# Order of the fillers at the opening of a gather-bound kernel, half of a top-64 moved among the first dots, and one unit's query products eight picks later

## The reference, cut to what matters

```
q = (h @ w_query)                          # 8 heads x 2 halves x 128
s1, s2 = q[:, :, 0] @ keys1.T, q[:, :, 1] @ keys2.T
# top 16 of each half, top 16 of their 256 sums -> 16 expert ids and softmax gates per head
u = exp_u[e_idx];  act = gelu(einsum('thkd,td->thk', u, h))
x += einsum('thk,thkd->td', gate * act, exp_v[e_idx])
```

## Time and profile before

| what | value |
|---|---|
| median of 3 runs | 1145.67 us |
| the profiled execution | 1144.68 us |
| its span | 1142.9 us |
| TensorE busy / VectorE / ScalarE / GpSimd | 75% / 69% / 40% / 47% |
| gather queue (q0): bytes, share of the 16 DMA engines' span | 402.68 MB, 83.8% |
| queue of SyncE (q1) | 52.87 MB, 11.5% |
| all reads and writes, mean | 400 GB/s |

### The profile page before, as it was taken

One profiled execution on the slowest core, in us unless ns is written; L12 is line 12 of the kernel. 1 busy time (PEld: TensorE's weight loads), 2 busy tenths in 40 slices (PEclk: granted clock), 3 DMA queues, 4 the chain that ended last, 5 costly groups with the idle time before them and its releaser, 6 DMA issues.

```text
span 1142.9 us, 12079 instructions
## 1 busy us (share of the span) xinstructions
PE 858.6 (75%) x3879; PEld 396.1 (35%) x3884; DVE 784.3 (69%) x2005; ACT 453.6 (40%) x1423; POOL 539.9 (47%) x437
## 2 busy tenths in 40 slices
PE   8999988997896858685586777576766675656566
PEld 6748743443232424242243342133223222211111
DVE  2325877876677778986666786757877767667544
ACT  2121444333443434543564663343343333333334
POOL 0002444553555645563553554555564555465452
PEclk9999999999998988998888998799788779887869
DMA  9902999999999999999999999999999999999996
GB/s 375 410 2 73 418 425 426 426 425 429 426 402 424 426 429 426 425 401 415 425 427 425 425 427 428 419 427 427 426 426 427 427 426 428 427 426 428 427 427 274
DMA packets 66791, 456.60 MB, mean 400 GB/s; under 512 B 8227, under 2 KB 10019, under 8 KB 15526
## 3 DMA queue, kind: packets, MB, share of 16 engines
q0 software_dynamic: 55888, 402.68, 83.8%
q1 hardware_dynamic: 10694, 52.87, 11.5%
q10 hardware_dynamic: 144, 0.26, 0.1%
HBM read 451.49 MB, written 3.24 MB: 398 GB/s over the span
## 4 chain that ended last, share of the span: by engine, by line
DMA 45%; PE 29%; DVE 13%; POOL 5%; ACT 4%; issue 4%; SPq 0%; POOLq 0%; DVEq 0%
DMA rows<-in_uv,ids 32%; PE ps L598 28%; DMA wt<-in_uv,ids 9%; DVE rows L2042 6%; POOL rows L537 2%; POOL work L520 1%; DMA rows<-in_w_qi 1%; DMA wt<-in_uv,last_ids 1%; DVE wt L2042 1%; ACT wt L1249 1%; ACT work L1249 1%; DMA wt<-in_w_q 1%; ACT wgt L1249 1%; POOL wt L537 1%; PE ps L601 1%
## 5 line engine op out<-in xcount | busy, mean ns | idle before, releaser
L537 POOL DMA_INDIRECT rows<-in_uv,ids x352 | 401.8, 1141 | 439.2 <-PE ps L598 355.4
L598 PE MATMUL ps<-rows,work 128*64 128x512 f32 x1416 | 409.1, 706 | 240.9 <-ACT work L1249 240.5
L2042 DVE CUSTOM_DVE_ANT_0 rows<-rows,wt 128x1024 f32<-128x1024 f32 x226 | 276.7, 1225 | 162.3 <-DMA rows<-in_uv,ids 161.0
L1249 ACT ACTIVATE zact<-zdot 128x1 f32<-128x1 f32 x354 | 71.4, 202 | 485.7 <-DVE zdot L2042 485.1
L598 PEld LDWEIGHTS ps<-rows,work 128*64 128x64 f32 x1416 | 95.9, 151 | 471.8 <-ACT work L1249 333.8
L598 PE MATMUL ps<-wt 128*128 128x128 f32 (+6 forms) x719 | 198.4, 484 | 31.0 <-ACT wt L1249 29.5
L2042 DVE CUSTOM_DVE_ANT_0 rows<-rows,masks 128x1024 f32<-128x1024 f32 x128 | 156.2, 1223 | 67.9 <-DMA rows<-in_uv,ids 66.9
L598 PEld LDWEIGHTS ps<-wt 128*128 128x128 f32 (+2 forms) x724 | 98.8, 188 | 111.0 <-issue 62.1
L1249 ACT ACTIVATE work<-pair,wgt 128x64 f32<-128x64 f32 x354 | 123.1, 348 | 11.6
L1249 ACT ACTIVATE wgt<-zact,gates 128x1 f32<-128x1 f32 x354 | 104.3, 295 | 11.5
L598 PEld LDWEIGHTS ps<-work,wt 128*128 128x128 f32 (+1 forms) x664 | 82.5, 198 | 50.4 <-issue 49.9
(11 more groups left out here) (178 smaller groups left out, 722.9 us busy)
## 6 DMA issues: line engine op xcount, KB each, us to landing
wt<-in_w_q SPq DMA_DIRECT2D x7, 2048.0 KB, 12.0
rows<-in_uv,ids POOLq DMA_INDIRECT x352, 14.3
rows<-in_w_out SPq DMA_DIRECT2D x2, 2048.0 KB, 32.7
wt<-in_w_out SPq DMA_DIRECT2D x2, 2048.0 KB, 12.0
wt<-in_ckv SPq DMA_DIRECT2D x16, 256.0 KB, 11.6
x<-in_x SPq DMA_DIRECT2D x5, 512.0 KB, 8.3
rows<-in_w_qi SPq DMA_DIRECT2D x1, 2048.0 KB, 13.1
wt<-in_w_qa SPq DMA_DIRECT2D x1, 2048.0 KB, 13.1
```

Of the source, the lines that this page charges most:

```text
L537: pool.indirect_dma_start(row[s], None, a["uv"], bass.IndirectOffsetOnAxis(ap=ids[:, own(n // KP).start + n % KP:own(n // KP).start + n % ...
L598: return nc.tensor.matmul(out, lhsT, rhs, start=start, stop=stop)
L1249: return nc.scalar.activation(*args, **kw)
L2042: V.tensor_tensor_reduce(row[s][:, 0:D], row[s][:, 0:D], h2r[t][:, n % 2, :], 1.0, 0.0, ALU.mult, ALU.add, zdots[s]).then_inc(dotted, 1)
```

## The change

Six edits. The opening on TensorE: `index_queries` counts single products instead of groups of 8; the first transpose of `h2_t` is split in two halves, and its wait for ScalarE's square moves to the two copies; `spread_out(0)` goes ahead of `dots_1(3)`; the four `later_qa` are interleaved with the first four sums (`add_experts(0)` to `(6)`), the last of them last; `y_start(0)` goes to tick 12. ScalarE weighs 8 picks around the two copies instead of 6. VectorE runs four of the eight top-64 rounds ahead of the dots and one after each of the dots 0 to 3. Attention of tile 1 starts one or two ticks later on three engines. Unit 7's query products go from ticks 64 to 70 (a quarter each) to tick 72 (all at once), their copy from pick 75 to 77; the index dots b = 4 and 5 of tile 2 from tick 68 to 70 with their relus; ids of units 5 and 6 are taken one pick later.

```diff
-        AHEAD, HURRIED, FAST = (1, 2, 15, 16), (2, 3, 8, 16), (2, 3, 16, 17, 18)
+        AHEAD, HURRIED, FAST = (1, 2, 15, 16), (2, 3, 7, 8, 16), (2, 3, 16, 17, 18)
 
         def q_at(u):
-            return {2: 8, 3: 10, 4: 20, 8: 88, 16: 224, 17: 230}.get(u, 16 * u - 48)
+            return {2: 8, 3: 10, 4: 20, 7: 72, 8: 88, 16: 224, 17: 230}.get(u, 16 * u - 48)
...
+            def h2_t0(e):
+                pe.wait_ge(gained, e + 1)
+                for c in range(4 * e, 4 * e + 4):
+                    last = tr(ps[:, 3 * e, (c % 4) * P:(c % 4 + 1) * P], h2[:, c * P:(c + 1) * P])
+                if e:
+                    last.then_inc(h2t_ps, 1)
...
-            index_queries(1, 6, 0, 1)
-            h2_t(0)
-            index_queries(1, 6, 1, 2)
+            h2_t0(0)
+            index_queries(1, 6, 0, 3)
+            h2_t0(1)
+            index_queries(1, 6, 3, 7)
             query(0)
-            index_queries(1, 6, 2, 3)
+            index_queries(1, 6, 7, 9)
             query_scores(0)
-            index_queries(1, 6, 3, 4)
+            index_queries(1, 6, 9, 32)
             pe.wait_ge(gb_sb, 1)
-            index_queries(2, 7, 0, 1)
+            index_queries(2, 7, 0, 4)
             pe.wait_ge(qi_sb, 2)
             pe.wait_ge(wz_set, 2)
             dots_1(0)
             dots_1(1)
             dots_1(2)
             sums_1(0)
+            spread_out(0)
             dots_1(3)
             sums_1(1)
-            spread_out(0)
             sums_1(2)
             sums_1(3)
-            index_queries(2, 7, 1, 4)
+            index_queries(2, 7, 4, 32)
             query(1)
-            later_qa(0)
             query_scores(1)
             pe.wait_ge(qi_sb, 3)
-            y_start(0)
             add_experts(0)
+            later_qa(0)
+            add_experts(2)
             later_qa(1)
-            add_experts(2)
+            add_experts(4)
             pe.wait_ge(scored, 2)
             later_qa(2)
+            add_experts(6)
             later_qa(3)
-            add_experts(4)
...
             def attention_1():
+                yield from until(6)
                 scores_1(0)
-                yield from until(6)
+                yield from until(8)
                 scores_1(1)
-                yield from until(14)
+                yield from until(12)
+                y_start(0)
+                yield from until(16)
                 prob_t1(0)
...
-                    yield from until(56 + 3 * b)
+                    yield from until(70 if b == 4 else 56 + 3 * b)
...
-            for n in range(4, 6):
+            for n in range(4, 8):
                 weigh(n)
             later_qa(1)
...
-            for r in range(0, TOPK[1], 8):
+            for r in range(0, TOPK[1] // 2, 8):
                 whole(score_round(score1, r, TOPK[1], 0))
                 whole(score_round(score1, r, TOPK[1], 1))
-            set_bias(bias1, score1)
...
-                    yield from until(spread_at(u) + (3 if u > 1 else 4))
+                    yield from until(spread_at(u) + (4 if u in (1, 5, 6) else 3))
                     spread_take(u)
 
             def attention_1():
-                yield from until(8)
+                for r in range(TOPK[1] // 2, TOPK[1], 8):
+                    whole(score_round(score1, r, TOPK[1], 0))
+                    yield from score_round(score1, r, TOPK[1], 1)
+                set_bias(bias1, score1)
+                yield from until(10)
```

More of the change, by code:

```diff
@@ L628, in keys_values, with index_queries @@
                 natural(t, w_kv, 6 + t % 2, NKV).then_inc(kv_ps, 1)
[L630 to L635, removed]
+            def index_queries(t, bank, i0, i1):
+                for i in range(i0, i1):
+                    j, c = divmod(i, KC)
+                    last = mm(ps[:, bank, j * P:(j + 1) * P], w_qi[:, c, j * P:(j + 1) * P], hT(t, c), c == 0, c == KC - 1)
+                if i1 == 4 * KC:
                     last.then_inc(qi_ps, 1)
@@ L646, in _ @@
             pe.wait_ge(w_in["qi"], 16)
-            index_queries(0, 4, 0, 2)
+            index_queries(0, 4, 0, 16)
             norm_t(1)
-            index_queries(0, 4, 2, 3)
+            index_queries(0, 4, 16, 24)
             norm_t(2)
-            index_queries(0, 4, 3, 4)
+            index_queries(0, 4, 24, 32)
             keys_values(1)
@@ L866, in y_start @@
                 for e in range(2):
-                    last = mm(ps[:, Y_BANK[t] + e, :], ident[:], x[:, t, e * 512:(e + 1) * 512], True, False)
+                    last = mm(ps[:, Y_BANK[t] + e, :], ident[:], x[:, t, e * 512:(e + 1) * 512], t > 0, False)
                 last.then_inc(y_init, 1)
@@ L880, in add_experts @@
                         s = ring(n + j)[0]
-                        last = mm(ps[64 * j:64 * j + 64, Y_BANK[n // (HP * KP)] + e, :], diag[s], row[s][:, D + e * 512:D + (e + 1) * 512], False, stop)
+                        last = mm(ps[64 * j:64 * j + 64, Y_BANK[n // (HP * KP)] + e, :], diag[s], row[s][:, D + e * 512:D + (e + 1) * 512], n == 0, stop)
                 last.then_inc(acc, 1)
@@ L1145, in attention_1 @@
             def attention_1():
+                yield from until(6)
                 scores_1(0)
-                yield from until(6)
+                yield from until(8)
                 scores_1(1)
-                yield from until(14)
+                yield from until(12)
+                y_start(0)
+                yield from until(16)
                 prob_t1(0)
-                yield from until(18)
+                yield from until(20)
                 values_1(0)
                 prob_t1(1)
-                yield from until(22)
+                yield from until(24)
                 values_1(1)
@@ L1241, in _ @@
                     y_start(n // (HP * KP))
-                if n > 4:
+                if n > 6:
                     add_experts(n, n % (HP * KP) == HP * KP - 2)
@@ L1311, in h2_take @@
                 act.wait_ge(h2t_ps, t + 1)
+                if t == 0:
+                    act.wait_ge(sqd, H2_STAT[0] + 1)
                 if t > 0:
@@ L1437, in background @@
             def background():
-                yield from until(11)
+                yield from until(13)
                 exps_1(0)
                 exps_1(1)
-                yield from until(19)
+                yield from until(21)
                 prob_t1(0)
-                yield from until(22)
+                yield from until(24)
                 values_1(0)
                 prob_t1(1)
-                yield from until(25)
+                yield from until(27)
                 values_1(1)
@@ L1463, in background @@
                         square(H2_STAT[1], x[:, 1, :], h2)
-                    yield from until(59 + 6 * (b // 2) + b % 2)
+                    yield from until(59 + 6 * (b // 2) + b % 2 + (2 if b in (4, 5) else 0))
                     relu_2(b)
@@ L1576, in _ @@
                 t = n // (HP * KP)
-                if n > 5:
+                if n > 7:
                     weigh(n)
@@ L1718, in h2_take @@
                 dve.wait_ge(h2t_ps, t + 1)
+                if t == 0:
+                    dve.wait_ge(sqd, H2_STAT[0] + 1)
                 if t > 0:
@@ L1893, in next_spreads @@
                 for u in range(1, UNITS):
-                    yield from until(spread_at(u) + (3 if u > 1 else 4))
+                    yield from until(spread_at(u) + (4 if u in (1, 5, 6) else 3))
                     spread_take(u)
             def attention_1():
-                yield from until(8)
+                for r in range(TOPK[1] // 2, TOPK[1], 8):
[3 more added lines that the diff above has]
+                yield from until(10)
                 yield from row_max(1, [ps[:, b, :].rearrange("p (j n) -> p j n", j=2) for b in (1, 2)], 0, 4)
-                yield from until(10)
+                yield from until(12)
                 yield from row_max(2, [ps[:, b, :].rearrange("p (j n) -> p j n", j=2) for b in (0, 3)], 4, 4)
-                yield from until(15)
+                yield from until(17)
                 yield from scale_probs(1, prob1[:, 0, :, :], 0, 4)
```

6 lines of the change are left out of this document (1 added, 5 removed).

## The result

The changed kernel took 1157.43 us (median of 4 runs, 1155.61 to 1160.92), the kernel before 1145.91 in the same comparison (4 runs, 1145.54 to 1146.6). The ratio is 1.0105 with a 95% interval of 1.0091 to 1.0119: it is slower by about 11.5 us. The forecast was 1151.1, with a range from 1142.5 to 1154.5. The profiled span is 1155.6 against 1142.9, 12.7 longer.

A forecast was written before the change was run, and what follows sets the result against it. From the first gather on, a fixed number of bytes at 427 GB/s bounds the kernel; only stream start and empty DMA queues move the end. Opening +7.0 and mid-kernel -1.6 give +5.4, median 1151.1 us, range 1142.5 to 1154.5.

The forecast's parts named there:

- Start of the stream: First gathers: spread at 105.8, gather 0 at 106.9 and its data at 108.7, 2.5 us earlier; bounds 2 to 3.
- small holes of 0.6 and 0.5 at gathers 12 and 14: DMA queue empty 0.6 us before gather 12's data at 141.1 and 0.5 before gather 14's at 146.5.
- Up to add 4: TensorE's opening: add 0 at 123.7, add 4 behind ScalarE's copy at 137.1, slab 1 issued at 148.2 instead of 139.82.
- The landing: Load of slab 1: 9.4 us from issue at 148.2 to 157.6, with TensorE 5.2 us idle.
- query(2) and gather 18: After slab 1: query(2) 3.7 + 1.7 us, gather 18 at 166.9, queue empty 7.4 us from 161.3; bounds 3.0 to 8.
- Opening in all: Sum of the opening: -2.5 + 0.6 + 0.5 + 7.4 + 1.0 = +7.0 us.
- Mid-kernel: Hole at 336 to 340 closes as gather 78 goes at 327.3 instead of 331.03: 1.6 us back.
- the queue covers all of the opening: Faster rival: gather 18's data ready by 161.3, the two small holes gone as well: 1141.6 us; chance 20%.
- the halfway case: Rival at slab 1: it lands in 6.7 us, the clock holds, empty 3.0 instead of 7.4: 1146.7 us; chance 14%.
- The rival above the forecast: VectorE's late ids and maxima delay gathers 22 and 24 by 2 to 3 us, or query(7) opens a hole: 1153.5; 12%.

The follow-up runs named there:

- the top-64 in one piece: The changed kernel with all eight rounds of tile 1's top-64 ahead of the dots, as before: 1157.1 us, ratio 1.0100 to the kernel before.
- the slab alone late: The kernel before with one wait more, so SyncE issues slab 1 only behind add 8: 1155.79 us, ratio 1.0089.
- the dummy products: The kernel before with the mid-kernel edits and 7 unread bf16 products behind each pair's add in ticks 112 to 126: 1146.13 us, ratio 1.0002.
- the kernel with the early scores: The changed kernel with the four later_qa at their old places and scores_1(1) at tick 6 instead of 8: 1144.02 us, ratio 0.9985 to the kernel before.
- the early `later_qa`: The changed kernel with the four later_qa back at their old places: 1144.21 us, ratio 0.9983 to the kernel before.
- query(2) behind add 10: The changed kernel with query(2) at tick 10, query(3) and unit 2's scores at tick 12: 1148.3 us, ratio 1.0024 to the kernel before.

## Why the prediction was right in kind and wrong in size

**Start of the stream.** Forecast: spread at 105.8, gather 0 at 106.9. Measured: 105.89 and 106.90. The times were right, but counting them as -2.5 in the sum was not safe: alone, the early start brings nothing, since gather 12 is bound by TensorE's work up to add 4. In the sum this stood as small holes of 0.6 and 0.5 at gathers 12 and 14. The window 140 to 144 shows 2.2 us lost, and 132 to 144 together 3.6. One reason is in the next paragraph: add 4 came 1.7 late, and gather 12 with it (141.04 for 139.3).

**Up to add 4.** Add 0 came at 123.70, as forecast, but took 3.06 instead of the 1.87 of my sum, and the `later_qa` behind it 4.24 instead of 3.6. The windows of the kernel after say why:

```profile
124.00:126.00 2.00, 2.00 (x8) 0.47 (x4) 1.93 (x10) 1.08 (x4) 0.00 (x0) 0.59 1.02 422
126.00:128.00 2.00, 2.00 (x6) 1.10 (x5) 1.95 (x7) 0.00 (x0) 0.94 (x1) 0.55 1.01 426
```

The granted clock is 0.59 and 0.55, near the lower level of 1.2 GHz, behind the idle times of 0.6 and 2.34 us that I had forecast myself. I counted a slower clock at query(2) and not here, on the row in which adds kept it after 2.48 us. Add 4 then came at 138.80 for 137.1, behind ScalarE's copy and its weighs as forecast (136.50, then two weighs), and the slab at 149.94 for 148.2. This term of the sum was 1.7 us too small.

**The landing.** Forecast 9.4, measured 11.84, so 2.4 too small in this execution. I had reasoned that a short queue of gathers leaves the slab a larger share. It did get one, but late. The bytes of each queue show it: between the issue at 149.94 and 153.7 no packet of the slab moved, only 1.4 MB of gathers issued before it. From 154 to 159 the slab had 1.88 MB of 2.11. In each of the seven kernels with a late slab its first packet moved 3.6 to 3.8 us after the issue, in the others 1.0 to 2.4 (in the kernel before 2.0). Besides, the rate fell. A window of the kernel after, behind the issue of the slab:

```profile
148.00:154.00 6.00, 5.60 (x35) 2.93 (x33) 2.32 (x6) 2.86 (x11) 0.72 (x1) 1.00 1.00 370
```

At a share of 1.00 the engines moved 370 GB/s where they otherwise move 427. But it is no property of the order: with the top-64 in one piece, the same gathers at nearly the same times (within 1.2 us) and the same issue of the slab, the landing took 9.98 and these 6 us moved 427. The last 0.1 MB of the slab was also slower, some 2.6 us against 1.4. Over all kernels with a late slab the landing ranged from 9.75 to 12.01. I took a value below all of them.

In the prediction I weighed a rule of the Trainium skill (DMA: Bandwidth & Descriptors, the section on queues, rings and completion order): round-robin between the queues that have work, packet by packet. I took it as equal halves of the bytes, 9.8 us or less, and left out the time before the first packet. Both were wrong. The kernel with the slab alone late has gathers queued all the time, and there the queues had, from 153 to 160 (packets, MB, share of the engines; q0 are the gathers, q1 is the slab):

```profile
q1 hardware_dynamic: 130, 1.92, 64.1%
q0 software_dynamic: 139, 1.01, 34.1%
```

By packets it is nearly one for one, as the rule has it; but a packet of the slab has 14.8 KB on average and one of a gather 7.3, so the slab gets two thirds of the bytes. What sets the wait of 3.6 us and the slow end is not shown here.

**query(2) and gather 18.** query(2) took 5.44 for the 5.4 forecast, with the clock lost as taken from the earlier trace rows. Gather 18 went at 171.00 for 166.9: 1.7 of the issue and 2.4 of the landing make the 4.1. (With the top-64 in one piece it went at 170.15, with a shorter landing and a slower query.) The queue ran dry at about 164.4, 3 us later than forecast, since the stream had already lost more on the way; so about 9 us were empty for 7.4. It restarted slowly (102 GB/s in 172 to 174), which I had counted for gather 0 and not here. Slab 2 came at 179.11 for 175, and ahead of it stands another thin place, 344 GB/s in 176 to 180.

**Opening in all.** Forecast +7.0, measured 12.2. By windows of 4 us, after minus before: the start gave 2.3 (2.5 forecast), the holes at 132 to 144 cost 3.7 (1.1), the thin rate of 144 to 160 1.0 (nothing), the hole ahead of gather 18 and the thin place behind it 9.7 (160 to 180; 8.4 forecast). So the steps that failed are sizes, not the path: add 0 and the `later_qa` behind it put at full clock, which made add 4 and the slab 1.7 late, and the landing put at 9.4, which took 11.84. The mechanism of the forecast is shown from both sides: the slab alone late costs 10.1, the old order of `later_qa` takes the loss away, and moving the waiting products behind add 10 takes most of it away with the slab still late. The clock is 3.3 of it and ScalarE's order 1.8; both act through the same chain, so the parts overlap and are not to be added.

**Mid-kernel.** Forecast -1.6, measured nothing in the changed kernel. The step that failed is the one that took the closing of one hole for a gain. The hole did close. But between 448 and 500 the kernels with these edits lose 0.9 to 3.1 us each (eleven of them, the changed one 2.3), those without 0.0 to 1.1 (five, the kernel before 0.4). Four pairs of kernels differ in these edits alone, and with them the time is 0.2, 0.6, 0.7 and 1.5 us lower on ratios (the changed kernel's pair 0.6), but within each pair the intervals overlap. A gain below the forecast is possible, and not shown. The slower clock was excluded as the main cause of the later loss by the dummy products (2.7 us lost with them, 2.6 at 460 to 472 without). What it is stays open.

**The rivals.** That the queue covers all of the opening (20%) and the halfway case (14%) didn't happen: the first needed gather 18's data at 161.3, and the gather was only issued at 171.00; the second needed a landing of 6.7 us, and it took 11.84. The rival above the forecast named VectorE's late ids and maxima; the row maxima did come late (168.89, behind 13.22 us of waiting for TensorE), but behind TensorE, as a result of the same chain, and with the `later_qa` back the loss is gone though the order on VectorE is the same.

## What to carry to other kernels

In a kernel that streams at the rate of its DMA engines, look at each load whose issue a change moves, and at what stands behind its consumer in the written order: here a load 9.4 us later cost 10.1 us where the engine that frees the stream's buffers waited for it in order, and 9 us came back when the release went ahead of that wait. Put the consumer behind the next release, or put work that needs nothing between the consumer and its predecessor (here that took the opening loss from 5.1 to 3.6, which the time didn't resolve). An earlier start counts only if the first reuse of a buffer moves with it, and a hole that closes only if the windows behind it stay full.

## What the runs showed of the hardware

- The DMA share does not tell the rate. A share of 1.00 went with 370 GB/s in 148 to 154, and 1.01 with 356 in the window 464 to 468 of the kernel with the early scores.
- The landing of one 2.10 MB load beside gathers took from 9.75 to 12.01 us with its issue at 147 to 152, and 9.98 or 11.84 in two kernels with the same order of issues. Issued at 138 to 141 it took 9.86 to 11.28 in eight kernels; three kernels with the opening of the kernel before had 9.98, 9.86 and 10.66. A range for it has to be some 2 us wide.
- Two DMA queues that both had work shared the engines by packets (130 to 139), not by bytes (1.92 to 1.01 MB): the queue with the larger packets got more.
- After waiting, TensorE's query products took 5.44 us after 2.42 idle in one kernel (the early `later_qa`; granted clock 0.50 in 150 to 152) and 3.81 after 2.38 in another (query(2) behind add 10; 1.00 in 160 to 164). Adds kept their time after 2.48 and lost 1.1 us after 0.6 and 2.34. An idle time of this length alone doesn't decide it, and both outcomes belong in the range.
